# Cross-attention in halves between its projections, waits for half a weight, and one-hots ahead of a branch: one change to a whole-model kernel on one core

## The chip, the cores and the metric

The kernel runs on one core of a Trainium2 chip. The core has a matrix engine (PE, TensorE), three engines for element-wise work (DVE, VectorE; ACT, ScalarE; POOL, GpSimd), a queue engine that issues transfers here (SP, SyncE), and 16 DMA engines. The metric is the device time of one launch in microseconds; times of several launches are given as their median.

## The reference, cut to what matters

Two layers of a hybrid block, then one block with a mixture of experts, all in float32; 256 tokens of 1024 values.

```python
h = x
for l in range(2):
    mix = hybrid_mixer(h, ...)               # recurrence and windowed attention
    h = layer_norm(A * h + mix, ...)
    h = layer_norm(A * h + cross_attention(h, mem, cq_w[l], ckv_w[l], co_w[l]), ...)
    h = layer_norm(A * h + swiglu(h, ffn_wi[l], ffn_wo[l]), ...)

def cross_attention(u, mem, cq_w, ckv_w, co_w):      # 4 heads of 256, 256 rows of mem
    q = (u @ cq_w).reshape(B, S, 4, 256)
    k, v = split(mem @ ckv_w)
    s = einsum('bshd,bmhd->bhsm', q, k) * 256 ** -0.5
    o = einsum('bhsm,bmhd->bshd', softmax(s), v)
    return o.reshape(B, S, 1024) @ co_w

# second block, once
x = x + g_a * merge(neighbourhood_attention, spatial_gate) @ w_out
t = rms(x) * (1 + scale) + shift
# 4 groups of 4 experts: the best group, in it the two best experts, with their weights
for e in range(16):
    out += gate[:, e] * ((silu(t @ w1[e]) * (t @ w3[e])) @ w2[e])
x = x + g_f * out
```

## The kernel before

**Order of work.** Each engine has a `Queue`: the program appends instructions to it, and the order in which it appends them is the order in which the engine runs them. An instruction carries the tokens (semaphore values) that it waits for. So an engine that waits at one instruction holds back all behind it.

**Weights.** All weights stream in as units of 1 MB (128 rows of 2048 values) in the order of a plan (`stream_plan`). SP issues their transfers to three `raw` buffers as these come free (`emit_dma`, L304), and two more, `landing`, are added late. Products are made to float32 precision from two parts: `split_half` (L320) makes, for 1024 of the 2048 columns at a time, a high part on ACT (`whs`, a copy to a reduced type) and a low part on DVE (`wls`, the rest), so a unit takes two such halves, and there are three places for split units. Activations are kept in two parts too (`P0h`, `P0l`, `P1h`, `P1l`), and `mm3` makes one product out of three: high by high, high by low, low by high. When PE has used a unit, `release` (L377) frees its place and appends the next halves to ACT and DVE (`pump`), unless the state `slow` or `hold` is set. `take` gives a GEMM its unit with the token to wait for: up to here the tokens of both halves, from its first product on.

**GEMMs and side work.** `gemm_tm` (L474) and `gemm_fm` (L512) run over units and tiles. After each tile they call `tick` (L388), which steps a generator in the list `side`, if there is one; this is how other work is put between the tiles. With `slow` set it also appends one half of a weight (`feed`). `finish_side` runs what is left of the generators.

**Cross-attention** (`cross`, L1052). Queries come from the two GEMMs of `cq_w`, two heads each. The generator `attend` (L1072) has three steps: `scores(t, hp)` makes scores and softmax for the rows of half t and two heads, `turn(hd)` transposes the weights of a head, `weigh(hd)` sums the values and splits the result for `co_w`. Copies go to ACT and DVE in turn. Before, the generator is run to its end between `cq_w` and `co_w`:

```python
            for c in range(2):
                gemm_fm("cq_w", P0, N["t"], (2 * c, 2 * c + 1), q_evac(c), by_unit=True)
...
            at = attend()
            next(at)
            side.append(at)
            finish_side()
```

**Second block.** `merge_evac` (L1614) takes the second half of `w_out_2`, adds the residual and makes the normalized rows `xn_`, for which DVE waits for a power on POOL. `f_fm` transposes them and splits them for the router and the experts; in its `early` form it returns `low(n)`, which makes the low parts later. The router's logits and the choice of experts follow on all engines, and at the end of it the counts of tokens per expert, their offsets, and for each token its two places in the sorted rows (`first`, `second`). A flag then sets a branch: where no expert has more than 128 tokens, the sparse way (`sparse`, L1792) runs. In it `gather` (L1809) makes one-hot matrices `Pall` of the places, two instructions for each half of the tokens, and with 32 products in eight banks brings the tokens into the order of the experts. Then come `up` and `down` for each expert.

## Time and profile before

| | |
|---|---|
| runs | 1680.62 us median of 3 (1676.35 to 1683.83) |
| profiled execution | 1681.34 us, its span 1679.4 us |
| mean granted clock of PE | 0.981 |
| PE busy | 1596.6 us (95%), 8036 products |
| PE's weight loads | 1303.4 us (78%) |
| DVE busy | 1151.0 us (69%), 1617 instructions |
| ACT busy | 903.9 us (54%), 1377 instructions |
| POOL busy | 79.7 us (5%) |
| DMA | 339.35 MB, mean 202 GB/s |
| chain that ended last | PE 70%, DVE 15%, ACT 8%, DMA 3%, issue 3% |

A row of a timeline names the line that issues the instruction, often that of a helper: L199 is a product, L203 a transpose, L207 a copy or function on ACT, L211, L215 and L219 are element-wise work on DVE, L222 a reduction, L225 a copy on DVE. A product of two float32 operands that are not split (scores and sums) shows as two records. `bank` is one of the eight PSUM banks, `tail` and `arena` are shared regions (in the cross-attention keys and values, queries and softmax). The granted clock is a share of full speed, 2.4 GHz. The releaser behind an arrow is what the engine waited for last.

### The profile page before, as it was taken

What the parts mean: (1) busy time and instruction counts of PE and PEld (TensorE: products, weight loads), DVE (VectorE), ACT (ScalarE), POOL (GpSimd) and SP (SyncE); (2) the same over time, 40 slices, a digit from 0 to 9 for tenths busy, and PEclk for the clock granted to TensorE, in tenths of its full rate; (3) what the DMA queues carried; (4) which work ended last, traced back from release to release, by engine and by line L of the source; (5) the groups of instructions that cost most, each with busy time, mean ns of one, the idle gap of its engine ahead of it and who ended that gap; (6) DMA issues with size and microseconds to landing.
All of it is one profiled execution on the core that took longest, in us unless ns stands there. A gap on an engine that the chain in (4) does not pass through costs nothing.

```text
span 1679.4 us, 20455 instructions
## 1 busy us (share of the span) xinstructions
PE 1596.6 (95%) x8036; PEld 1303.4 (78%) x8036; DVE 1151.0 (69%) x1617; ACT 903.9 (54%) x1377; POOL 79.7 (5%) x75
## 2 busy tenths in 40 slices
PE   7999999989999999989999899999989969999997
PEld 7987788776888789878878667888767758777786
DVE  7457655657545584667566478866664669999997
ACT  5466443435444364764434254544353448888885
POOL 0010000001000000100000000000200000000005
PEclk9999999999999999999999999999999879999999
DMA  7445234535654454542356278874440318999995
GB/s 286 177 153 198 89 112 158 194 126 211 242 198 177 149 202 175 204 172 86 116 200 226 75 259 296 315 257 175 150 169 26 119 63 302 364 374 369 370 371 177
DMA packets 52202, 339.35 MB, mean 202 GB/s; under 512 B 7835, under 2 KB 8477, under 8 KB 13316
## 3 DMA queue, kind: packets, MB, share of 16 engines
q1 hardware_dynamic: 48932, 331.79, 53.7%
q0 software_dynamic: 3168, 6.20, 1.0%
q8 instruction: 65, 1.06, 0.3%
q14 instruction: 37, 0.30, 0.1%
HBM read 332.82 MB, written 10.49 MB: 204 GB/s over the span
## 4 chain that ended last, share of the span: by engine, by line
PE 70%; DVE 15%; ACT 8%; DMA 3%; issue 3%; POOL 1%; ACTq 0%; DVEq 0%; SPq 0%
PE bank L199 66%; DVE wls L211 6%; PE bank L203 4%; ACT whs L207 3%; DMA raw<-in_ws_dram 3%; ACT arena L208 1%; DVE arena L211 1%; DVE sm L222 1%; ACT P1h L1847 1%; DVE h L211 1%; DVE arena L219 1%; POOL sm L231 1%; DVE arena L844 1%; ACT arena L207 1%; DVE arena L215 1%
## 5 line engine op out<-in xcount | busy, mean ns | idle before, releaser
L211 DVE TENSOR_TENSOR wls<-raw,whs 128x1024 fp32r<-128x1024 f32 x442 | 523.5, 1227 | 243.4 <-ACT whs L207 242.8
L207 ACT ACTIVATE whs<-raw 128x1024 fp32r<-128x1024 f32 x442 | 443.2, 1051 | 276.1 <-PE bank L199 193.3
L199 PE MATMUL bank<-whs,P1h 128*128 128x512 f32 (+1 forms) x732 | 291.2, 398 | 5.2 <-DVE P1l L1849 2.0
L199 PE MATMUL bank<-whs,P1l 128*128 128x512 f32 (+1 forms) x732 | 285.5, 390 | 0.0
L199 PE MATMUL bank<-wls,P1h 128*128 128x512 f32 (+1 forms) x732 | 285.1, 390 | 0.0
L199 PE MATMUL bank<-whs,P0h 128*128 128x512 f32 (+1 forms) x640 | 257.6, 402 | 6.3 <-DVE P0l L211 2.5
L199 PE MATMUL bank<-whs,P0l 128*128 128x512 f32 (+1 forms) x640 | 250.2, 391 | 0.0
L199 PE MATMUL bank<-wls,P0h 128*128 128x512 f32 (+1 forms) x640 | 250.1, 391 | 0.0
L199 PEld LDWEIGHTS bank<-whs,P1h 128*128 128x128 f32 x732 | 138.4, 189 | 36.2 <-DVE P1l L211 3.6
L199 PEld LDWEIGHTS bank<-whs,P1l 128*128 128x128 f32 x732 | 138.3, 189 | 29.2
L199 PEld LDWEIGHTS bank<-wls,P1h 128*128 128x128 f32 x732 | 138.4, 189 | 26.9
L199 PEld LDWEIGHTS bank<-whs,P0h 128*128 128x128 f32 x640 | 122.1, 191 | 40.3 <-issue 6.7
L199 PEld LDWEIGHTS bank<-whs,P0l 128*128 128x128 f32 x640 | 121.7, 190 | 25.8
L199 PEld LDWEIGHTS bank<-wls,P0h 128*128 128x128 f32 x640 | 122.0, 191 | 23.9 <-issue 0.7
L207 ACT ACTIVATE arena<-bank 128x256 f32<-128x256 f32 (+1 forms) x131 | 59.8, 463 | 82.6 <-PE bank L199 67.6
L208 ACT ACTIVATE arena<-arena,sm 128x128 f32<-128x128 f32 (+2 forms) x80 | 40.1, 502 | 92.7 <-DVE sm L215 92.7
L203 PE MATMUL bank<-ident,arena 128*128 128x128 f32 x386 | 64.6, 287 | 19.9 <-DVE arena L225 8.7
L199 PE MATMUL bank<-P0h,whs 128*128 128x256 f32 x256 | 74.3, 290 | 4.1 <-DVE wls L211 4.1
L231 POOL TENSOR_TENSOR sm<-sm,mhalf 128x1 f32<-128x1 f32 (+1 forms) x30 | 24.3, 811 | 1089.8 <-DVE sm L215 952.4
L203 PEld LDWEIGHTS bank<-ident,arena 128*128 128x128 f32 x386 | 49.9, 151 | 31.8 <-ACT arena L207 8.4
L199 PE MATMUL bank<-P1h,whs 128*128 128x256 f32 x256 | 73.7, 288 | 0.0
L199 PE MATMUL bank<-P0h,wls 128*128 128x256 f32 x256 | 73.1, 286 | 0.0
(267 smaller groups left out, 2497.1 us busy)
## 6 DMA issues: line engine op xcount, KB each, us to landing
raw<-in_ws_dram SPq DMA_DIRECT2D x264, 1024.0 KB, 4.9
landing<-in_ws_dram SPq DMA_DIRECT2D x38, 1024.0 KB, 7.1
lnb<-in_ln_g_dram SPq DMA_DIRECT2D x6, 512.0 KB, 5.8
lnb<-in_ln_b_dram SPq DMA_DIRECT2D x6, 512.0 KB, 6.5
ydram<-arena POOLq DMA_DIRECT2D x4, 512.0 KB, 11.8
mid<-in_bias_dram SPq DMA_DIRECT2D x1, 2048.0 KB, 7.6
h<-in_x_dram SPq DMA_DIRECT2D x2, 512.0 KB, 4.0
lnb<-in_mem_dram SPq DMA_DIRECT2D x1, 1024.0 KB, 13.1
```

Of the source, the lines that this page charges most:

```text
L199: return PE.put(lambda e: e.matmul(out, lhsT, rhs, start=start, stop=stop, skip_group_check=skip), w, inc)
L203: return PE.put(lambda e: e.transpose(out, in_, ident[0:n, 0:n]), w, inc)
L207: return AC.put(lambda e: e.activation(out, in_, func, bias=bias, scale=scale), w)
L208: return AC.put(lambda e: e.activation(out, in_, func, bias=bias, scale=scale, accum_out=acc), w)
L211: return VE.put(lambda e: e.tensor_tensor(out, a, b, op), w)
L215: return VE.put(lambda e: e.tensor_scalar(out, a, s1, None, op0), w)
L219: return VE.put(lambda e: e.scalar_tensor_tensor(out, a, s, b, op0, op1), w)
L222: return VE.put(lambda e: e.tensor_reduce(out, a, AX.X, op), w)
L231: return GP.put(lambda e: e.tensor_tensor(out, a, b, op), w)
L844: v3 = VE.put(lambda e, k=k: e.tensor_tensor_scan(xc[:, k, :], ra[:, k, :], gi[:, k, :], 0.0, ALU.mult, ALU.add), [v2])
L1847: a = AC.put(lambda g, hi=hi, at=place_of: g.activation(hi, at(AC), ACT.Copy, bias=0.0, scale=1.0), [[T["all", k] for k in range(k0, k1)], ...
```

## The change

It has four parts.

1. **Start.** The first half of `x` is loaded ahead of the identity and the condition, the second half behind them.
2. **Halves of units.** A unit's token becomes two, and `half_of` gives a product that reads the first half of the unit the first token alone. All GEMMs use it.
3. **Cross-attention.** `attend` is in `side` while the second GEMM of `cq_w` runs, so the scores of the first two heads lie between its tiles. The rest is in another order, and the last two sums come behind the first tile of `co_w`.
4. **Router.** Two low parts of `f_fm` are appended in DVE's wait for POOL, with `hold` set until `f_fm` is done, and one more half of a weight is appended behind it. The four instructions for `Pall` stand ahead of the branch, the cast of the offsets behind them; `gather` makes the 16 products of the first half of the tokens first, which wait for its one-hots alone, then those of the second.

```diff
@@ split_half, take
-                split_tok[n] = [split_tok[n], tok]
+                split_tok[n] = [[split_tok[n]], [tok]]
...
+        def half_of(tok, kk, per):
+            return tok[0] if isinstance(tok, list) and 2 * kk < per else tok
...
+        xr = ins["x"].rearrange("a (t p) d -> p (a t) d", p=128)
+        c_h = [load(h[:, 0, :], xr[:, 0, :], s="d_h0")]
         c_ident = load(ident[:, :], ins["ident"], s="d_ident")
         c_cond = load(sm[:, 640:656], ins["cond"], s="d_cond")
-        xr = ins["x"].rearrange("a (t p) d -> p (a t) d", p=128)
-        c_h = [load(h[:, t, :], xr[:, t, :], s=f"d_h{t}") for t in range(2)]
+        c_h.append(load(h[:, 1, :], xr[:, 1, :], s="d_h1"))
@@ gemm_tm
-                            part(w, slice(None), kk), first, closes and kk == per - 1, tok,
+                            part(w, slice(None), kk), first, closes and kk == per - 1, half_of(tok, kk, per),
...
@@ cross
-            for c in range(2):
-                gemm_fm("cq_w", P0, N["t"], (2 * c, 2 * c + 1), q_evac(c), by_unit=True)
-            xfree = PE.last()
...
-                for hp in range(2):
-                    for t in range(2):
-                        scores(t, hp)
-                        if t:
-                            yield
+                for t in range(2):
+                    scores(t, 0)
+                    yield
+                yield
                 turn(0)
                 turn(1)
+                for t in range(2):
+                    scores(t, 1)
+                for hd in range(2):
+                    weigh(hd)
+                    oT[0].append(X[("o", hd)])
+                turn(2)
+                turn(3)
                 yield
-                for hd in range(2, 6):
-                    weigh(hd - 2)
-                    if hd < 4:
-                        turn(hd)
-                    if hd % 2:
-                        yield
-
+                for hd in range(2, 4):
+                    weigh(hd)
+                    oT[1].append(X[("o", hd)])
+                yield
+
+            oT = [[], []]
+            gemm_fm("cq_w", P0, N["t"], (0, 1), q_evac(0), by_unit=True)
+            finish_side()
             at = attend()
-            next(at)
             side.append(at)
-            finish_side()
+            gemm_fm("cq_w", P0, N["t"], (2, 3), q_evac(1), by_unit=True)
+            xfree = PE.last()
...
             gemm_tm("co_w", src, lambda i: i, res_evac(rs, 0))
+            finish_side()
@@ merge_evac, router
+                    if t:
+                        fT[0][2](0)
                     xn_[t] = ts(xs[:, t, :], h[:, t, :], smv(o + 5, 1), None, ALU.mult, None, g, Q["ph"])
+                    if t:
+                        fT[0][2](1)
+                        state["slow"], state["hold"] = False, True
...
-        for n in range(2):
-            fT[0][2](n)
         fT = [fT[0][0], f_fm(1, False)[0]]
+        state["slow"], state["hold"] = True, False
...
-        feed(2)
+        feed(3)
...
-        v_off = vcopy(offi[:, :], begins, d_)
...
         v_place = tt(second, second, first, ALU.subtract, a_, d_)
+        p_at = []
+        for t in range(2):
+            p_ = ts(Pall[:, t, :], count, first[:, t:t + 1], None, ALU.is_equal, None, n_, v_place, Q["ph"])
+            p_at.append(stt(Pall[:, t, :], count, second[:, t:t + 1], f32(Pall[:, t, :]), ALU.is_equal, ALU.add, p_))
         v_slot = ts(slot, slot, -1.0, None, ALU.add, None, v, v_place)
+        v_off = vcopy(offi[:, :], begins, v_slot)
@@ gather
-                for t in range(2):
-                    p_ = ts(Pall[:, t, :], count, first[:, t:t + 1], None, ALU.is_equal, None, n_, v_place, start)
-                    p_ = stt(Pall[:, t, :], count, second[:, t:t + 1], f32(Pall[:, t, :]), ALU.is_equal, ALU.add, p_)
...
                 for k in range(8):
-                    for i in range(4):
-                        t, p = i // 2, i % 2
-                        m = mm(banks[k][:, :], rows[p][:, t, k * 128:(k + 1) * 128], Pall[:, t, :], i == 0, i == 3,
-                               p_, rows_tok, bankfree[k], inc=(i == 3))
+                    for p in range(2):
+                        mm(banks[k][:, :], rows[p][:, 0, k * 128:(k + 1) * 128], Pall[:, 0, :], p == 0, False,
+                           p_at[0], rows_tok, bankfree[k])
+                for k in range(8):
+                    for p in range(2):
+                        m = mm(banks[k][:, :], rows[p][:, 1, k * 128:(k + 1) * 128], Pall[:, 1, :], False, p == 1,
+                               p_at[1], inc=(p == 1))
```

On PE, before, this stands between the last products of `cq_w` (names with P1) and the first of `co_w` (names with P0): four score blocks of four products, then transposes and sums in turn.

```order
L199 MATMUL bank<-P1l,whs 128x256
L199 MATMUL bank<-P1h,wls 128x256
L199 MATMUL bank<-tail,arena 128x256 x16
L203 MATMUL bank<-ident,arena 128x128 x8
L199 MATMUL bank<-arena,tail 128x256 x4
L203 MATMUL bank<-ident,arena 128x128 x4
L199 MATMUL bank<-arena,tail 128x256 x4
L203 MATMUL bank<-ident,arena 128x128 x4
L199 MATMUL bank<-arena,tail 128x256 x8
L199 MATMUL bank<-whs,P0h 128x512
```

Two of these blocks have moved ahead of this place, and two of the four sums behind it, as the next pieces show.

In the changed kernel the first score block stands on PE behind the first tile of `cq_w`'s second GEMM, and the second block stands likewise one tile later.

```order
L199 MATMUL bank<-P1l,whs 128x256
L199 MATMUL bank<-P1h,wls 128x256
L199 MATMUL bank<-tail,arena 128x256 x4
L199 MATMUL bank<-P1h,whs 128x256
L199 MATMUL bank<-P1l,whs 128x256
```

A block that stood behind the GEMM is now inside it, and the GEMM's other tiles come behind it.

Behind that GEMM the two other score blocks stand between two pairs of transposes, with the first two sums ahead of the second pair.

```order
L199 MATMUL bank<-P1l,whs 128x256
L199 MATMUL bank<-P1h,wls 128x256
L203 MATMUL bank<-ident,arena 128x128 x8
L199 MATMUL bank<-tail,arena 128x256 x8
L199 MATMUL bank<-arena,tail 128x256 x8
L203 MATMUL bank<-ident,arena 128x128 x8
L199 MATMUL bank<-whs,P0h 128x512
```

Eight products of scores and eight of sums are left here. The eight other products of sums now stand after the first 12 products of `co_w`.

On DVE, in the cross-attention of layer 0 (L225 `arena<-bank` copies queries, `wls` is the low half of a weight, L222, L215 and L228 belong to one softmax), the softmaxes of the first two score blocks have moved ahead among the weight halves.

```order
 L225 COPY arena<-bank 128x512
-L211 TENSOR_TENSOR wls<-raw,whs 128x1024 x4
-L225 COPY arena<-bank 128x512
-L211 TENSOR_TENSOR wls<-raw,whs 128x1024 x2
+L211 TENSOR_TENSOR wls<-raw,whs 128x1024 x2
+L222 TENSOR_REDUCE sm<-bank 128x2
+L215 TENSOR_SCALAR sm<-sm 128x2
+L228 RECIPROCAL sm<-sm 128x2
+L215 TENSOR_SCALAR arena<-arena,sm 128x256 x2
+L211 TENSOR_TENSOR wls<-raw,whs 128x1024 x2
+L222 TENSOR_REDUCE sm<-bank 128x2
+L215 TENSOR_SCALAR sm<-sm 128x2
```

Each softmax now has a pair of weight halves ahead of it on DVE.

On DVE, at the end of the router, this is the difference from the flag on (`Pall` are the one-hots; L2071 and L2073 read the flag and branch).

```order
 L222 TENSOR_REDUCE sm<-sm 128x2 x2
 L211 TENSOR_TENSOR sm<-sm 128x2
-L215 TENSOR_SCALAR sm<-sm 128x32
-L2071 TENSOR_LOAD flag
-L2071 ISA x2
-L2073 COMPARE_AND_BRANCH
 L215 TENSOR_SCALAR Pall<-arena,sm 128x512
 L219 SCALAR_TENSOR_TENSOR Pall<-arena,sm,Pall 128x512
 L215 TENSOR_SCALAR Pall<-arena,sm 128x512
 L219 SCALAR_TENSOR_TENSOR Pall<-arena,sm,Pall 128x512
+L215 TENSOR_SCALAR sm<-sm 128x32
+L225 CAST offi<-sm 128x16
```

The one-hots, which stood behind the branch, stand ahead of the last small operation and of the cast of the offsets, which the branch now follows.

## Rows read from the trace of the kernel before

**Rows 1.** PE's waits. Engine, buffer, line <- releaser: us in all, times, longest.

```profile
PE bank L199 <- ACT arena L207: 6.1, 2, 3.0
PE bank L199 <- DVE wls L211: 6.0, 5, 4.1
PE bank L199 <- DVE Pall L219: 5.7, 1, 5.7
PE bank L199 <- ACT arena L208: 5.5, 4, 2.1
```

**Rows 2.** Timeline, SP at the start: start us, us, instruction, xcount.

```profile
0.73 0.40 SPq L245 DMA_DIRECT2D ident<-in_ident_dram  x1
...
1.66 0.90 SPq L245 DMA_DIRECT2D h<-in_x_dram  x2
```

**Rows 3.** Timeline, PE at the start; [idle before <-releaser].

```profile
5.23 1.94 PE L203 MATMUL bank<-ident,h 128*128 128x128 f32 x8 [5.23 <-DMA h<-in_x_dram]
...
13.88 0.55 PE L199 MATMUL bank<-P0h,whs 128*128 128x256 f32 x1 [4.12 <-DVE wls L211]
```

**Rows 4.** Timeline, DVE at the start.

```profile
11.38 5.77 DVE L211 TENSOR_TENSOR wls<-raw,whs 128x1024 fp32r<-128x1024 f32 x5 [0.25 <-ACT whs L207]
```

**Rows 5.** Timeline, ACT at the start.

```profile
14.83 2.00 ACT L207 ACTIVATE whs<-raw 128x1024 fp32r<-128x1024 f32 x2 [0.48 <-DMA raw<-in_ws_dram]
```

**Rows 6.** Timeline, PE in the cross-attention of layer 0.

```profile
344.40 0.28 PE L199 MATMUL bank<-P1l,whs 128*128 128x256 f32 x1
344.52 0.28 PE L199 MATMUL bank<-P1h,wls 128*128 128x256 f32 x1
344.64 3.62 PE L199 MATMUL bank<-tail,arena 128*128 128x256 f32 x16
...
354.81 1.04 PE L203 MATMUL bank<-ident,arena 128*128 128x128 f32 x8
358.88 3.53 PE L199 MATMUL bank<-arena,tail 128*128 128x256 f32 x8 [3.04 <-ACT arena L207]
...
364.86 3.73 PE L199 MATMUL bank<-arena,tail 128*128 128x256 f32 x16
368.24 0.58 PE L199 MATMUL bank<-whs,P0h 128*128 128x512 f32 x1
368.66 0.39 PE L199 MATMUL bank<-wls,P0h 128*128 128x512 f32 x1
```

**Rows 7.** Timeline, DVE in the cross-attention of layer 0.

```profile
336.45 0.69 DVE L225 COPY arena<-bank 128x512 f32<-128x512 f32 x1
...
348.27 0.69 DVE L222 TENSOR_REDUCE sm<-bank 128x2 f32<-128x512 f32 x1
...
350.98 0.69 DVE L222 TENSOR_REDUCE sm<-bank 128x2 f32<-128x512 f32 x1
```

**Rows 8.** Timeline, PE in the cross-attention of layer 1.

```profile
920.41 3.62 PE L199 MATMUL bank<-tail,arena 128*128 128x256 f32 x16
```

**Rows 9.** Timeline, DVE in the cross-attention of layer 1.

```profile
912.68 0.68 DVE L225 COPY arena<-bank 128x512 f32<-128x512 f32 x1
```

**Rows 10.** Timeline, PE at the border of two units, feed-forward of layer 0.

```profile
456.29 0.39 PE L199 MATMUL bank<-whs,P1l 128*128 128x512 f32 x1
456.52 0.39 PE L199 MATMUL bank<-whs,P0h 128*128 128x512 f32 x1
```

**Rows 11.** Timeline, PE in the gather (its 1st and 14th product).

```profile
1373.49 0.80 PE L199 MATMUL bank<-Pall,P0h 128*128 128x512 f32 x1 [5.70 <-DVE Pall L219]
...
1379.21 0.40 PE L199 MATMUL bank<-Pall,P0l 128*128 128x512 f32 x1
```

**Rows 12.** Timeline, DVE from the router to the one-hots.

```profile
1369.69 0.16 DVE L211 TENSOR_TENSOR sm<-sm 128x2 f32<-128x2 f32 x1
...
1370.98 0.49 DVE L215 TENSOR_SCALAR Pall<-arena,sm 128x512 fp32r<-128x512 f32 x1 [0.91 <-DVE sm L215]
```

**Rows 13.** Timeline, ACT ahead of the router.

```profile
1354.50 1.51 ACT L207 ACTIVATE arena<-bank,sm 128x128 f32<-128x128 f32 x4 [2.57 <-DVE P1l L211]
```

**Rows 14.** Windows: us, busy (xcount) PE, PEld, DVE, ACT, POOL; PEclk, DMA share, GB/s.

```profile
360.00:369.00 9.00, 9.00 (x42) 7.52 (x41) 2.67 (x4) 2.66 (x5) 0.00 (x0) 0.89 0.00 0
...
1374.00:1386.00 12.00, 10.02 (x33) 7.63 (x32) 6.38 (x20) 4.45 (x7) 0.00 (x0) 0.78 0.01 1
```

15 lines of the change are left out of this document (8 added, 7 removed).

## The prediction

> **What bounds the kernel now.** I read the table of engines first, then PE's waits, then the timelines of the places that the diff touches. PE is busy for 1596.6 of 1679.4 us, so the change can win only where PE stands still (82.8 us) or runs at the low clock. The reader should see in PE's waits that no single one is large and that the diff goes to four of the larger: `wls` 6.0, `Pall` 5.7, and `arena` from ACT 6.1 and 5.5, both inside the two cross-attentions [rows 1]. With the 5.2 at the very start [rows 3] that is 28.5 us, the most that could go. In the feed-forward and the experts PE runs nearly without a gap, so what is saved ahead of them is saved at the end.
>
> **Start.** SP issues the identity at 0.73 and the first half of `x` as its third transfer, at 1.66 [rows 2]. PE waits for `x` until 5.23 [rows 3], 3.57 after the issue. Issued first, at 0.73, it is there at 4.30: 0.93 earlier. The identity goes out some half a microsecond later and, being much smaller, is not what is late.
>
> PE's first product is at 13.88, after a wait of 4.12 for the low half of the first weights [rows 3]. DVE makes five such halves in 5.77, from 11.38 [rows 4]: one every 1.13. With the wait halved, PE goes on after the first of them, 1.13 earlier; six products then cover the second. ACT's first wait for a weight DMA is at 14.83, for the third unit [rows 5], so nothing shows that the 0.93 is lost to a DMA; if the first unit landed only when ACT took it, it is. Ends: 0 and 2.1. I take 2.1, as no row shows such a wait.
>
> **Cross-attention, twice.** Before, four score blocks, four transposes and four weighted sums stand alone between two GEMMs. In layer 0 PE starts them at 344.64 and reaches `co_w` at 368.24, in 23.6 [rows 6]. In it PE waits 5.8, which is half of 6.1 + 5.5 [rows 1], and the first weighted sum takes 3.53 where two later ones take 3.73 together [rows 6]: 1.65 lost to the low clock. So 7.4 at most can be won per layer.
>
> After, two score blocks stand inside the second `cq_w` GEMM. They push its end back by the 3.62 that they take [rows 6]; call that end T'. A new wait comes in: the first block needs all queries of the first GEMM, and DVE copies the last of them only at 336.45, for 0.69 [rows 7], behind layer-norm work. The second GEMM is 96 products of 0.12 [rows 6], so it starts at 333.1, and its first quarter ends at 336.0. PE waits 1.1 there. In layer 1 the same reckoning from 920.41 gives 911.8, against a copy that ends at 913.4 [rows 8, 9]: 1.6. Behind this wait stand the other three quarters of the GEMM.
>
> From T', DVE first makes two weight halves, done 3.6 after T' (as 348.27 is to 344.64 [rows 6, 7]), then a copy of 0.69, then two softmaxes of 2.71 (348.27 to 350.98 [rows 7]): T' + 9.7. PE meanwhile has two transposes (1.04 [rows 6]), two score blocks (3.62) and two weighted sums (3.73): T' + 8.4. So it waits 1.3 for the softmax, transposes (1.04), and waits 0.4 more, because the splits of the two sums (0.69 each) stand behind that softmax on DVE. `co_w` starts at T' + 11.2, does one tile (2.75), does the last two sums (3.73), and goes on at T' + 17.7. Before, that point lay at 23.6 + 2.75 = 26.4 after the old end of the GEMM; now it lies at 3.62 + 1.1 + 17.7 = 22.4: 4.0 saved. In layer 1 the longer first wait leaves 3.5. **Together 7.5**, between 0 and 14.8 (no wait left, no slow sum). The weight splits that now stand between the softmaxes wait for the same GEMM as before; they are ahead of their use by a unit, so their shift costs nothing.
>
> **Weights by halves elsewhere.** Apart from the start, four waits for `wls` are left, 6.0 - 4.1 = 1.9 in sum [rows 1]. The first half is there 1.13 before the second, so most of it goes. I take 1.5 of 0 to 1.9, as some of them stand ahead of an attention stage that waits for ACT in any case. The change adds 100 waits on PE ahead of the branch, and almost none behind it. A wait that is already met costs nothing that can be seen: at the border of two units, where the names change from P1 to P0 and a wait stands, the products stay 0.23 apart [rows 10]. So I cost these at nothing; if PE's stream didn't cover them, rival 4 says what they take. The Trainium skill, "TensorE: Matmul & The Clock Gate", puts into the table at its head that PE pulls weight loads ahead of products that still run, and prices 128 columns at an estimated 0.107 us (section on LDWEIGHTS). A load that must wait for its own half can't be pulled ahead, so by that rule 100 waits would give back 10.7, the sum would be 2.5 instead of 13.2, and the time 1678; the rows at the border speak against it.
>
> **Router and one-hots.** PE waits 5.70 for the four one-hot instructions and begins the gather at 1373.49 [rows 11]. DVE has their inputs at 1369.69 + 0.16, does one small operation, crosses the branch (0.91), and makes them from 1370.98 on [rows 12], in 2.5 for four. After, they follow at once, from about 1369.8 (the cast of the offsets, a tenth, now comes behind them), and the gather needs only two of the four to begin: 1371.0 to 1371.1, which is 2.4 earlier. The other two are done 1.25 later, and 16 products stand between. Against this stands a moved split. Two low parts go into DVE's wait for POOL, and ACT need not wait 2.57 for them [rows 13]; the evacuation of the second transposes starts some 0.6 earlier. But one weight half, 1.0 on ACT, now stands ahead of the copies of the router's logits, and ACT has no gap from there on: the logits come 0.3 to 0.4 later. Net 2.1, between 0.3 and 2.5. The gate sums on DVE now come behind the one-hots and the branch; they end about when the first copy of the gather is wanted, so I cost them at nothing, and at a copy's 0.7 if they are late.
>
> **Sum.** 2.1 + 7.5 + 1.5 + 2.1 = 13.2. The profiled execution took 1681.34, so it would take 1668.1. It stands 0.7 above the median of the runs, 1680.62, so I forecast **1667.4**. About 0.5% (8.4 us) is what a measurement of this kernel can tell from no change.
>
> **Rivals.**
>
> 1. *The softmax is not hidden.* If in each layer one more unit's split (two halves, 2.3) and a copy (0.7) get in ahead of the second softmax, 3 are lost twice, the cross-attentions give 1.5, and the time is 1673.4. For it: ACT and DVE work in order, and these splits wait for PE. Against it: the first two softmaxes have two or three quarters of a GEMM, 5.8 to 8.6, before their use.
>
> 2. *The start is set by a DMA.* Then the 2.1 become 0 to 1.1, and the time 1668.4 to 1669.5. For it: the wait at 14.83 [rows 5]. Against it: it is the third unit that waits.
>
> 3. *The clock.* After a wait PE's products can come at half the rate: from 1373.49 the gather's first 13 steps take 5.7, 0.44 each instead of 0.23 [rows 11], at a mean granted clock of 0.78 [rows 14]. The change swaps one large gap for three smaller ones in each cross-attention. If each of the six is followed by 3.5 us (the slow sum [rows 6]) to 5.7 us at 1.2 GHz, half of that is lost each time, 10 to 17 in all: 1678 to 1685. **Slower than before** from 13.2 on, which is 2.2 for each gap. Against it: the old gaps were 5.8 in 10.6 us and left the clock at 0.89 behind them [rows 14]; the new ones are 1.1 to 1.6, 1.3 and 0.4, with 6 to 10 us of work between them.
>
> 4. *A wait inside a tile holds PE up.* The most that a first product costs in the rows is one step of 0.42 instead of 0.23 after other work (368.24 to 368.66 [rows 6]). At 0.19 for each of the 100 waits that is 19, and the time 1686; slower than before from 0.13 each. Against it: the border of two units [rows 10].
>
> **How the numbers follow.** The forecast has 0.63, rival 1 0.15, rival 2 0.10, rival 3 0.08, rival 4 0.04. Faster by over 0.5% means under 1672.2: most of the forecast's spread, rival 2 and a little of rival 1 make 0.69. Within 0.5%: most of rival 1, the low ends of 3 and 4, and the tail of the forecast, 0.25. Slower by over 0.5% needs 21.6 more than forecast, which is rivals 3 and 4 together or something that no row shows: 0.06. The range goes from 1661 (cross-attentions at 11 and the router at its end, with the runs' scatter of 3 below the median) to 1678 (rival 1, and the low end of rival 3).
>
> **What would show it.** PE's first product of weights lies near 11.8. In each cross-attention PE no longer waits for ACT's `arena`; it waits 1 to 1.6 ahead of the first score block and about 1.3 ahead of the third transpose. One wait for `Pall` of 3 to 3.5 is left instead of 5.7, and of the waits for `wls` about 3, at the start. The prediction would be wrong with score blocks that wait over 3 inside the GEMM, a granted clock under 0.85 in a cross-attention, steps over 0.3 inside weight tiles, or a gather whose evacuation waits for the gate sums.

## The result

| | before | change |
|---|---|---|
| median, with the ratio of the change to before | 1678.81 us (4 runs) | 1660.8 us (4 runs), 0.9888, interval 0.9859 to 0.9918 |
| the same, measured again (e12 below) | 1676.65 us (17 runs) | 1661.36 us (6 runs), 0.9895, interval 0.9872 to 0.9918 |
| profiled execution, its span | 1681.34, 1679.4 us | 1661.53, 1659.7 us |
| PE idle, span less busy time | 82.8 us | 68.5 us |

The change is faster by 1.1%, some 18 us; 13.2 were forecast, and the time lies just under the lower end of the range, 1661.0; the second measurement lies just inside it. These two rows of the page of the changed kernel answer to the table shown of before.

```profile
span 1659.7 us, 20348 instructions
...
PE 1591.2 (96%) x8036; PEld 1303.7 (79%) x8036; DVE 1149.8 (69%) x1617; ACT 903.1 (54%) x1377; POOL 79.9 (5%) x75
```

PE's waits of the changed kernel, in us in all, times and longest:

```profile
PE bank L203 <- DVE arena L215: 8.2, 4, 4.7
...
PE bank L203 <- DMA ident<-in_ident_dram: 4.2, 1, 4.2
...
PE bank L199 <- DVE Pall L219: 3.2, 1, 3.2
PE bank L199 <- DVE wls L211: 2.9, 1, 2.9
...
PE bank L203 <- DMA h<-in_x_dram: 1.2, 1, 1.2
```

Of the four waits in [rows 1], the two of the cross-attentions are gone, and `wls` and `Pall` have become one shorter wait each, as the forecast said. The first wait, 5.2 for `x`, is now 4.2 for the identity. New are 1.6 for the last softmax of each cross-attention (in the 8.2, which before were 4.6), and 1.2 for the second half of `x`.

To see where time goes, I lined up PE's instructions of each profile with those of before and took, at each place, how much earlier the same product starts. The table gives the growth of that lead (negative: time saved) from place to place, places in the time of before. The columns e1 to e5 are the experiments below; a stretch whose program an experiment leaves alone is a control.

| stretch of before | change | again (e12) | e1 start | e2 halves | e3 cross | e4 router | e5 experts |
|---|---|---|---|---|---|---|---|
| to 14, first weights | -1.64 | -1.81 | -0.57 | -1.24 | +0.06 | -0.06 | +0.24 |
| 312 to 390, cross-attention 0 | -3.89 | -5.25 | -0.04 | +0.15 | -5.33 | +0.14 | +0.06 |
| 390 to 689 | -0.55 | -0.49 | -0.06 | -0.58 | +0.06 | -0.09 | +0.17 |
| 689 to 874 | +3.38 | +3.43 | -0.08 | +1.53 | +2.97 | +1.02 | +1.54 |
| 888 to 968, cross-attention 1 | -5.37 | -5.37 | +0.10 | -0.14 | -5.17 | -0.07 | -0.02 |
| 968 to 991 | -1.36 | -1.37 | -0.52 | -1.38 | +0.01 | -0.47 | -0.52 |
| 991 to 1050 | -2.63 | -2.68 | -2.50 | -2.66 | +1.73 | -2.48 | -1.99 |
| 1050 to 1186 | -1.02 | -1.02 | 0.00 | -1.03 | 0.00 | 0.00 | 0.00 |
| 1186 to 1333 | -0.48 | -0.45 | -0.19 | -0.94 | -0.85 | -0.06 | -4.38 |
| 1333 to 1373, router | -2.06 | -2.02 | -0.02 | -0.20 | -0.08 | -1.98 | -0.22 |
| 1373 to 1390, gather, first expert | -2.06 | -2.08 | -0.02 | -0.04 | +0.04 | -2.03 | -0.09 |
| 1390 to 1671, experts | -1.98 | -1.78 | +0.33 | -1.97 | -0.18 | +0.10 | -1.81 |
| all else | +0.03 | -0.06 | -0.47 | +0.12 | -0.08 | -0.23 | -0.30 |
| whole, to 1671 | -19.63 | -20.95 | -4.04 | -8.38 | -6.82 | -6.21 | -7.32 |

Three lines are not the change's. From 991 to 1050 most kernels are 2.0 to 3.2 ahead of before, e4 and e5 among them, whose program is that of before up to 1300. There the one profiled execution of before lost time: DVE waited 1.39 for a weight.

```profile
1034.15 2.33 DVE L219 SCALAR_TENSOR_TENSOR arena<-raw,sm,arena 128x512 f32<-128x512 f32 x3 [1.39 <-DMA raw<-in_ws_dram]
```

In e1 DVE does not wait there. From 1186 to 1333 e5 gains 4.38 where it has nothing changed: over these 147 us the mean granted clock was 0.95 in its profile and 0.92 in that of before. And the loss from 689 to 874, where the diff changes only which half of a weight is waited for, is the clock's too. These are two windows of before, then the same of the change, with the granted clock in the column behind POOL:

```profile
745.00:775.00 30.00, 25.87 (x138) 20.57 (x137) 19.77 (x33) 16.00 (x45) 0.00 (x0) 0.94 0.22 74
815.00:835.00 20.00, 18.20 (x95) 14.98 (x94) 10.23 (x15) 6.99 (x10) 0.00 (x0) 1.00 0.31 108
```

```profile
745.00:775.00 30.00, 25.88 (x137) 20.80 (x137) 19.16 (x36) 14.59 (x42) 0.00 (x0) 0.89 0.27 104
815.00:835.00 20.00, 18.19 (x84) 14.81 (x84) 9.93 (x14) 8.89 (x12) 0.00 (x0) 0.91 0.30 110
```

Lower by 0.05 for 30 us and by 0.09 for 20, the clock takes some 3.3 us, which is the loss. Kernels without the new cross-attention have part of it: e2, 0.89 and 1.00, loses 1.5. What makes the clock fall there stays open. So a difference of two profiled executions means something only at a place that moves in every kernel with the edit and in none without it.

### The profile page after: what moved, and what is told of

The parts are those of the page before. It is cut to its first block, busy times and chain, and to the rows that moved or that the text cites. A ratio compares the mean times of both kernels' runs of the same rounds, so it can differ in the third digit from the quotient of the medians.

```text
span 1659.7 us, 20348 instructions
## 1 busy us (share of the span) xinstructions
PE 1591.2 (96%) x8036; PEld 1303.7 (79%) x8036; DVE 1149.8 (69%) x1617; ACT 903.1 (54%) x1377; POOL 79.9 (5%) x75
## 4 chain that ended last, share of the span: by engine, by line
PE 72%; DVE 17%; ACT 6%; DMA 2%; issue 2%; POOL 1%; SPq 0%; DVEq 0%; ACTq 0%
PE bank L199 68%; DVE wls L211 7%; PE bank L203 4%; ACT whs L207 2%; DMA raw<-in_ws_dram 2%; DVE h L211 1%; DVE arena L211 1%; ACT arena L208 1%; DVE sm L222 1%; POOL sm L231 1%; DVE arena L219 1%; DVE arena L849 1%; DVE arena L215 0%; ACT arena L207 0%; ACT L207 0%
```

## The experiments

### The four parts, each alone

The edits are the parts of the diff above, each put alone into the kernel before.

**e1, start.**

> Only the order of the loads at the start is changed. Theory A (each part is worth what its own place shows): PE's first transposes start near 4.2 instead of 5.23 and the first product of weights near 13.0 to 13.4 instead of 13.88, so 0.5 to 1.0 us are gained, ratio 0.9994 to 0.9997, which no timing can tell from 1. Rival B (the second half of x, now issued fourth, takes the gain back): the first product of weights stays within 0.3 of 13.88.

Measured: ratio 0.9991 (0.9975 to 1.0007). The first transposes start at 4.29, where PE now waits for the identity, and the second half of `x` is waited for by 0.87; the first product of weights comes at 13.31, 0.57 earlier. Theory A.

**e2, halves.**

> Only the waits for half a unit are put in. Theory A (place by place): the wait ahead of the first product of weights falls from 4.1 to 2.9 to 3.0, the four other waits for wls (1.9 in sum) go but are mostly met again at the next wait for an activation; the stage of the experts ends as many us after its first product as before, within 0.5; 1.5 to 3 us in all. Rival B (half waits are what shortens the expert stage by 2.0 and the stretch 980 to 1050 by 3.5 in the changed kernel): 5 to 8 us, with the expert stage 2.0 shorter. Rival C (100 more waits cost PE): slower than before by 5 or more, steps over 0.3 inside tiles.

Measured: ratio 0.9974 (0.9959 to 0.9990). By the table 1.24 at the start, 1.38 from 968 to 991 (0.5 of it in the controls too), 1.03 from 1050 to 1186, and 1.97 in the experts, to which 0.58 from 390 to 689 come. Theory A's "within 0.5" for the experts falls. Rival C falls: the first product of a second half, in the middle of a tile, keeps the step of 0.23. Rival B was right on the experts and wrong on 991 to 1050, which is an accident of before. Why half waits help in the experts is left to e5 and e13.

**e3, cross-attention.**

> Only the cross-attention is changed. Theory A: PE's waits in the two cross-attentions fall from 11.6 to 4 to 5 (the softmax of the last two score blocks 1.6, a split 0.4, each twice, and a query copy) and the slow weighted sum at 358.88 is gone: from the start of cq_w to the feed-forward 4 to 5.5 us less in each layer, 8 to 11 in all, ratio 0.9935 to 0.995. The stretch 980 to 1050 and the experts stay as before within 1. Rival B (the transfers that follow layer 1 come earlier against PE, so the 3.5 us of waits between 980 and 1050 go with this part): 12 to 14 us, ratio 0.992.

Measured: ratio 0.9952 (0.9934 to 0.9970). 5.33 and 5.17 are saved, 10.5 in all, within Theory A. Rival B falls, as 991 to 1050 does not shorten here; it is 1.73 longer, at a granted clock of 0.97 instead of 1.00.

**e4, router.**

> Only the low parts, the one-hots ahead of the branch and the order of the gather are changed. Theory A (the wait and the clock): PE's wait for Pall falls from 5.7 to 3.2, and the clock comes back within the gather, so the first expert's first products come at 0.23 and not at 0.43 as before: 4 to 5 us, ratio 0.997 to 0.9976. Rival B (the wait alone): 2 to 2.6 us, with steps of 0.43 behind the gather as before. Rival C: the expert stage behind it, where the transfers were busy 96% of the time, takes back what comes ahead of it: under 1 us at the end.

Measured: ratio 0.9984 (0.9969 to 1.0000). PE waits 3.2 for `Pall`; 1.98 are saved up to the gather, and 2.03 more up to the first expert. Theory A by the trace, and Rival C falls: what is saved ahead of the experts is still there at the end. The ratio is worth 2.7 us, with an interval from 0 to 5, and tells neither from Rival B. Windows of before (the gather's slow part, its rest with the wait behind it, the first expert) and of the change show the clock in the column behind POOL:

```profile
1373.40:1379.20 5.80, 5.71 (x13) 4.46 (x14) 3.64 (x19) 0.78 (x2) 0.00 (x0) 0.50 0.01 3
1379.20:1385.70 6.50, 4.53 (x20) 3.38 (x18) 2.94 (x5) 3.37 (x6) 0.00 (x0) 1.00 0.00 0
1385.70:1389.30 3.60, 3.58 (x9) 2.86 (x10) 3.57 (x5) 2.43 (x4) 0.00 (x0) 0.55 0.00 0
```

```profile
1357.90:1361.40 3.50, 3.50 (x8) 2.81 (x9) 2.35 (x10) 0.00 (x0) 0.99 (x2) 0.50 0.00 0
1361.40:1369.60 8.20, 5.95 (x25) 4.46 (x23) 5.60 (x18) 4.11 (x7) 0.00 (x0) 0.97 0.00 0
1369.60:1373.20 3.60, 3.54 (x15) 2.92 (x16) 3.60 (x6) 2.79 (x5) 0.00 (x0) 1.00 0.02 5
```

Before, PE stood still 5.7, then ran at 0.50 of full speed (1.2 GHz) for 5.8, and after the next wait, 2.0, it was granted 0.55 on the mean of 3.6 us. With the change it stands still 3.2 and runs at 0.50 for 3.5; after a next wait of 2.3 it is at full speed (2.4 GHz). The second slow stretch is there in every kernel with the old one-hots (before, e1, e2, e3, e5, e6, e13, e14) and in none with the new ones (change, e4, e7 to e12, e15, e16).

### What the router's part consists of

**e9, one-hots alone.** Added to before: the four instructions ahead of the branch; the gather as it was.

```diff
+            p_at.append(stt(Pall[:, t, :], count, second[:, t:t + 1], ...))   # ahead of the branch
...
                         m = mm(banks[k][:, :], rows[p][:, t, ...], Pall[:, t, :], i == 0, i == 3,
-                               p_, rows_tok, bankfree[k], inc=(i == 3))
+                               p_at[1], rows_tok, bankfree[k], inc=(i == 3))
```

> The kernel before with the one-hots ahead of the branch alone; the gather in its old order, waiting for all four of them, and no low parts. Theory A (the clock behind the gather depends on how long PE stood still ahead of it): the wait for Pall falls from 5.7 to 4.4 to 4.5, and the slow stretch behind the first expert's wait (1.7 to 2.0 us in the kernel before, gone in the four kernels with the whole change of the router) stays, so 1.2 us. Rival B (what clears it is that the products come in another order or earlier against something else): the slow stretch goes here too, 2.9 to 3.2 us.

Measured: ratio 0.9979 (0.9966 to 0.9993). Theory A falls on the clock: the wait is 1.3 shorter, as it said, but the slow stretch at the first expert is gone too, and 2.62 more are saved up to there. The windows are the gather's start and the first expert:

```profile
1369.90:1373.00 3.10, 3.10 (x7) 2.47 (x8) 1.84 (x12) 0.60 (x1) 0.99 (x2) 0.50 0.02 5
1381.10:1385.40 4.30, 4.28 (x19) 3.56 (x20) 4.08 (x6) 3.61 (x6) 0.00 (x0) 1.00 0.13 19
```

The ratio is worth 3.5 us, with an interval from 1.2 to 5.7, so the effect is the one of Rival B. But the order of the products is not what clears the second slow stretch. What has changed ahead of it is the length of the first standstill, 4.4 instead of 5.7, and of the slow stretch behind it; whether that is the cause, or that the products come earlier against something else, stays open.

**e7, without the low parts.** The change, but these lines as before:

```diff
-                    if t:
-                        fT[0][2](0)
...
+        for n in range(2):
+            fT[0][2](n)
...
-        feed(3)
+        feed(2)
```

> The changed kernel with the low parts and the weight half ahead of the router put back as before (two halves of a weight there, low parts behind the normalized rows). Theory A (the moved half costs more than the low parts give: 0.39 gained, 0.89 lost in the trace of the changed kernel): the first product of the gather comes 0.4 to 0.6 earlier, counted from the start of w_out_2's second half, and the time is 0.5 under the changed kernel's. Rival B (the low parts are worth the 0.6 that the prediction gave them, and the half is needed ahead of the gather): 0.3 to 1.5 over the changed kernel's.

Measured: ratio 0.9907 (0.9887 to 0.9927), 1661.44: the change's time. By the leads, low parts and moved half give 0.43 ahead of the router, take 0.86 in it, and give back 0.35 in the gather and 0.6 behind it: 0.5 for the change in all. That is near what a stretch wanders by where nothing is changed (-0.2 to +0.3 in the experts), and no timing can tell it, so neither theory is settled.

**e8, two orders changed.** The change with the second half of `x` third and two halves of a weight ahead of the router:

```diff
-        c_cond = load(sm[:, 640:656], ins["cond"], s="d_cond")
         c_h.append(load(h[:, 1, :], xr[:, 1, :], s="d_h1"))
+        c_cond = load(sm[:, 640:656], ins["cond"], s="d_cond")
...
-        feed(3)
+        feed(2)
```

> The changed kernel with the second half of x issued ahead of the condition, and with two halves of a weight ahead of the router instead of three (low parts as in the change). Theory A: PE's wait for the second half of x falls from 1.2 to 0.7 to 0.8, the router's logits come 0.9 earlier as ACT has one copy of 1.0 less ahead of them, and the unit whose half is left out is not needed until the first experts, whose wait for P1l is longer: 1.0 to 1.4 us under the changed kernel's time. Rival B (the half that is left out is met again by the first expert, which waits for it): 0.4 under it, all of it from the start.

Measured: ratio 0.9912 (0.9896 to 0.9929), and the start lost 1.2: the lead at the first product of weights is 0.42 instead of 1.64. Both theories missed ACT: its first instruction works on the condition, and now waits for that transfer until 7.05, with the copies of the first transposes queued behind it.

```profile
7.05 0.21 ACT L207 ACTIVATE sm<-sm 128x16 f32<-128x16 f32 x1 [5.04 <-DMA sm<-in_cond_dram]
7.17 1.07 ACT L207 ACTIVATE P0h<-bank 128x512 fp32r<-128x512 f32 x2
```

The missing half of a weight brings the logits 0.7 earlier; 0.4 of it is left at the first expert and 0.2 at the end.

### The cross-attention

**e6, sums ahead of co_w.** As e3, without the step between the transposes and the last sums:

```diff
                 turn(2)
                 turn(3)
-                yield
                 for hd in range(2, 4):
                     weigh(hd)
```

> As e3_cross, but all four weighted sums stand ahead of co_w. Theory A (the scores inside the GEMM hide the first softmax, and the late sums hide only the copy of the last transposes and the split of the first sums): the wait of 1.6 for the softmax stays, a new wait of 0.7 to 1.2 comes ahead of the third sum, and each layer gives 0.7 to 1.2 less than in e3_cross: 6 to 7.5 us where that gave 9 to 10 by its trace. Rival B (the late sums are most of the gain, as they give DVE time to split): 3 us in all, ratio 0.998.

Measured: ratio 0.9958 (0.9945 to 0.9972). 5.51 and 5.33 are saved, as much as in e3. Both theories fall: ahead of the third sum PE waits 0.25, not 0.7 to 1.2, and the 0.41 for the split ahead of `co_w` is gone. The late sums are worth nothing here, and the whole gain is that the first two score blocks lie in the GEMM and the rest is in another order.

**e10, query copies on ACT.**

```diff
-                    X[("q", f // 2)] = copy_by(j, qT[:, f:f + 2, :], ps, m, mend)
+                    X[("q", f // 2)] = copy_by(j if c else 0, qT[:, f:f + 2, :], ps, m, mend)
```

> The changed kernel with both query copies of cq_w's first GEMM on ACT. Theory A (the term of the query copy: only the second head's half of the first score block waits for DVE's copy): the first score block takes 1.54 from its start to the next tile in both layers, as the second one does, instead of 1.9 and 1.4 with a wait of 0.4; 0.4 in each layer, 0.8 in all, which no timing can tell. Rival B (ACT's copy comes later than DVE's, or holds up a weight half): the block waits 0.5 or more.

Measured: the first block takes 1.54 in both layers, without a wait. Theory A. The ratio, 0.9877 (0.9857 to 0.9896), lies within the interval of the change's.

**e11, weight halves behind the softmax.** e10 and:

```diff
                 for t in range(2):
                     scores(t, 0)
                     yield
+                state["hold"] = True
                 yield
...
                 turn(2)
                 turn(3)
+                state["hold"] = False
+                pump()
                 yield
```

> As e10, and the two weight halves that stand between the query copies and the third softmax come behind the last transposes. Theory A (these halves, 2.4 us on DVE, are why PE waits 1.6 for the last softmax): this wait falls to 0 to 0.4, the wait for the split (0.4) stays, and the slow stretch behind it in layer 0 (1.7 in the changed kernel) goes: 2.5 to 3.5 us under e10, near 1657. Rival B (the halves are then late for co_w's second unit or the splits of the last sums stand behind them): a new wait of 1 to 2 in co_w, and no gain.

Measured: ratio 0.9869 (0.9850 to 0.9888), 1655.9. Theory A for the waits: the one for the softmax falls from 1.61 to 0.20, that for the split stays at 0.41, and the layers save 7.28 and 7.45, which is 3.0 and 1.6 more than in e10. By the medians it is only 1.0 under e10 (1656.93), with intervals that overlap. PE at the third transpose, first in the change, then in e11:

```profile
356.63 0.88 PE L203 MATMUL bank<-ident,arena 128*128 128x128 f32 x6 [1.61 <-DVE arena L215]
357.92 0.47 PE L199 MATMUL bank<-whs,P0h 128*128 128x512 f32 x1 [0.41 <-DVE P0l L211]
358.23 0.51 PE L199 MATMUL bank<-wls,P0h 128*128 128x512 f32 x1
358.54 0.63 PE L199 MATMUL bank<-whs,P0l 128*128 128x512 f32 x1
358.96 0.63 PE L199 MATMUL bank<-whs,P0h 128*128 128x512 f32 x1
```

```profile
357.56 0.88 PE L203 MATMUL bank<-ident,arena 128*128 128x128 f32 x6 [0.20 <-DVE arena L215]
358.85 0.47 PE L199 MATMUL bank<-whs,P0h 128*128 128x512 f32 x1 [0.41 <-DVE P0l L211]
```

In the change the products of `co_w` behind these waits come 0.43 apart for a while (358.54 to 361.52), in e10 too; in e12 and e11 they come 0.23 apart. Its first tile takes 4.42 in the change and 2.84 in e12 (357.92 to 362.34, and 357.74 to 360.58), so 1.6 is lost, which is why the two profiles of the change differ in cross-attention 0. As e12 is the same program as the change, nothing shows that the edit of e11 clears this slow stretch. Between 14 and 312, ahead of its edit, the profile of e11 loses 2.7, with a granted clock of 0.93 instead of 0.97 from 160 to 210.

### Half waits or fewer conditions

**e5, half waits in the experts alone.**

> Waits for half a unit in the experts alone, up and down; all ahead of the branch as before. Theory A (the 2.0 us that the expert stage is shorter with half waits, 0.3 at each of seven places, come from the products of an expert that use a unit whose second half DVE has just made): 2.0 us from the first expert's first product to the end, nothing ahead of it, ratio 0.9988. Rival B (the expert stage is shorter because the units come into it earlier after all that was saved ahead): no change behind the first expert, ratio 1.000.

Measured: the expert stage is 1.81 shorter, with nothing ahead of it changed, so Theory A has the place. By timing it can't be told: ratio 1.0001 (0.9989 to 1.0012). But the cause it gives is wrong. The products that start sooner are the first of an expert's second stage, `whs,Pall`, and in both kernels what comes last for them is DVE's split of the hidden rows; the unit's halves are earlier instructions of DVE. In before DVE ends that split at 1450.11:

```profile
1449.69 0.42 DVE L211 TENSOR_TENSOR Pall<-bank,Pall 128x256 fp32r<-128x256 f32 x1
```

PE starts the product 0.25 later, 0.44 after the one ahead of it:

```profile
1449.92 0.39 PE L199 MATMUL bank<-whs,P1l 128*128 128x512 f32 x1
1450.36 0.47 PE L199 MATMUL bank<-whs,Pall 128*128 128x512 f32 x1
```

With half waits alone DVE ends the split at 1444.44, and PE starts 0.10 later, 0.28 after the product ahead:

```profile
1444.26 0.39 PE L199 MATMUL bank<-whs,P1l 128*128 128x512 f32 x1
1444.54 0.47 PE L199 MATMUL bank<-whs,Pall 128*128 128x512 f32 x1
```

The trace's semaphore records, which the timeline leaves out, show what stands between. Before, two separate wait instructions stand ahead of this product on PE's weight-load queue, one with one condition and one with two; with half waits there is none, and the load of the product's weights carries the wait itself. Over the whole run the separate wait instructions of PE fall from 258 to 151 in the change, which are the 107 instructions that its page counts less (20348 instead of 20455), though 100 products more have a wait.

Is it the conditions or the instructions that cost? Three other products of the stage have one separate wait in both kernels, with two conditions in before and with one in e5. The step is the same, 0.32 to 0.35. The first of them, before and with half waits:

```profile
1415.40 0.39 PE L199 MATMUL bank<-whs,P1l 128*128 128x512 f32 x1
1415.72 0.47 PE L199 MATMUL bank<-whs,Pall 128*128 128x512 f32 x1
```

```profile
1409.89 0.39 PE L199 MATMUL bank<-whs,P1l 128*128 128x512 f32 x1
1410.21 0.47 PE L199 MATMUL bank<-whs,Pall 128*128 128x512 f32 x1
```

So the price goes with the number of separate wait instructions, not with their conditions.

**e13, the condition alone.** In before, the latest token first, so that the older values of the same semaphore need no wait:

```diff
-                                part(w, slice(None), k, cols_), i == 0 and k == 0, i == 1 and k == 1, tok,
-                                T["hT", c], bankfree[b] if i == 0 and k == 0 else None, inc=(k == 1))
+                                part(w, slice(None), k, cols_), i == 0 and k == 0, i == 1 and k == 1, T["hT", c],
+                                tok, bankfree[b] if i == 0 and k == 0 else None, inc=(k == 1))
```

> The kernel before; only in an expert's second product the tokens stand in another order: the transposed hidden rows (DVE's latest value) first, the unit's halves, which are older values of the same semaphore, behind it, so that they need no wait of their own. PE waits for the whole unit as before. Theory W (a product that PE stands at pays 0.15 for a second condition in the wait ahead of it, and half waits gave 2.0 in the experts because they left one condition out): the expert stage is 1.5 to 2.2 shorter, as in e5, nothing ahead of it changes. Theory H (the half wait itself gave it, as PE need not wait for the second half): no change, within 0.3.

Measured: 2.30 from the first expert on, more than with half waits, and no half is waited for. Theory H falls. DVE ends the split at 1445.02, and the product starts 0.05 later, at a step of 0.24, next to the bare 0.23:

```profile
1444.83 0.39 PE L199 MATMUL bank<-whs,P1l 128*128 128x512 f32 x1
1445.07 0.50 PE L199 MATMUL bank<-whs,Pall 128*128 128x512 f32 x1
```

So where the operand is only just ready, two separate waits cost the step 0.21, one 0.10 to 0.12, and none 0.05 (e5) or 0.01 (e13, which has no separate wait there either); ten products of the stage read so in each of the three kernels, and three more, of before and e5, have the one. What sets 0.05 against 0.01 is open. A separate wait that was met long before costs nothing: before, 108 of 120 products of 512 columns behind one keep the step of 0.23. The time, ratio 0.9994 (0.9977 to 1.0010), can't show 2 us.

**e14, merged in before; e15, in the change; e16, in the best.** One value for each semaphore:

```diff
+    def flat(self, tokens, most):      # the latest value of each semaphore
...
     def wait(self, tokens):
-        for t in tokens:
...
-            sem, value = t
+        for sem, value in self.flat(tokens, {}).values():
```

> The kernel before, with the tokens of an instruction merged to one value for each semaphore, everywhere; PE's separate wait instructions fall from 350 to 62 (half waits alone: 185), ACT's from 400 to 326. Theory W: the expert stage 1.5 to 2.5 shorter, and where half waits alone had gained, at 968 to 991 (0.9) and 1050 to 1186 (1.0), this kernel gains nothing or little, as no half is waited for there; 2 to 4 us in all. Theory H: nothing in the expert stage, 0 to 1 us in all.

> The changed kernel with merged tokens; PE's separate wait instructions fall from 182 to 60. Theory W: most of those on PE's path went with the half waits, so 0.3 to 1.5 us under the changed kernel, in places with several producers (gather, router, attention). Theory H: the same time as the changed kernel within 0.5 in every stretch that the clock leaves alone.

> As e11 (query copies on ACT, weight halves behind the softmax), with merged tokens. Theory W: 0.3 to 1.5 under e11, ratio to the kernel before 0.985 to 0.988; Theory H: the ratio of e11, 0.987, within its interval.

Measured: e14 ratio 0.9973 (0.9963 to 0.9983), as much as half waits (0.9974) without one half wait: 2.44 in the experts, and 1.37 from 968 to 991, where Theory W expected little, but only 0.10 from 1050 to 1186 and nothing at the start. So of what half waits gave, the experts and most of 968 to 991 are fewer separate waits; the start and 1050 to 1186 are the half that needn't be waited for. On the change (e15, 0.9906, 0.9886 to 0.9926) and on e11 (e16, 0.9878, 0.9858 to 0.9897) merging is worth nothing that shows.

### The change again

**e12.**

> The changed kernel again, beside these. Theory A (the parts add up: 1.5 + 4.4 + 8.0 + 2.7 by the medians of the four parts alone): 15 to 18 us under the kernel before, ratio 0.9893 to 0.9911, and in the trace the first expert's products come at 0.23 from the start. Rival B (the profiled execution of the change was itself a lucky one): under 14 us, and the stretches that differ from the first profile are those of the clock.

Measured: ratio 0.9895 (0.9872 to 0.9918), 15.3 by the medians; the parts alone gave 0.6, 3.9, 6.0 and 1.9 by their own medians, 12.4, or by their ratios 1.5 + 4.4 + 8.0 + 2.7 = 16.6. Theory A, to within the intervals, which are some 3 us either way for each part. The profile differs from the first in the clock alone, by 1.4 in cross-attention 0.

## Why the prediction was wrong

It had the direction, and undershot by 5 us by the first measurement, by 2 to 4 by the second. Three of its steps failed: the wait for the query copy in the cross-attention, the price of met waits in the term of the halves, and the clock behind the gather, which it put at nothing. By its own steps:

- **Start, 2.1: measured 1.6 to 1.8.** The half wait gave what was said: PE waits 2.92 instead of 4.12. Of the 0.93 only half arrived. The first transposes come 1.04 earlier, but what they wait for is now the identity, which the prediction held to be "not what is late", and the second half of `x`, issued fourth, makes PE wait 1.19:

```profile
4.19 1.97 PE L203 MATMUL bank<-ident,h 128*128 128x128 f32 x8 [4.19 <-DMA ident<-in_ident_dram]
7.35 1.97 PE L203 MATMUL bank<-ident,h 128*128 128x128 f32 x8 [1.19 <-DMA h<-in_x_dram]
12.24 0.58 PE L199 MATMUL bank<-P0h,whs 128*128 128x256 f32 x1 [2.92 <-DVE wls L211]
```

- **Cross-attention, 7.5: measured 9.3 and 10.6 in the two profiles of the change.** The stretch behind the GEMM was worked out well: 1.61 for the softmax (1.3 forecast), 0.41 for the split (0.4), and `co_w` starts 11.06 after T' (11.2). The step that failed is the new wait for the query copy, "the first block needs all queries of the first GEMM". Only its second head does; for the first, ACT's copy is enough, and that ends at 329.5. In layer 0 the block begins while DVE's copy of the last queries still waits its turn; in layer 1 its second half waits 0.37:

```profile
328.87 0.60 ACT L207 ACTIVATE arena<-bank 128x512 f32<-128x512 f32 x1
334.43 2.25 PE L199 MATMUL bank<-tail,arena 128*128 128x256 f32 x8
334.82 0.68 DVE L225 COPY arena<-bank 128x512 f32<-128x512 f32 x1
...
910.50 1.13 PE L199 MATMUL bank<-tail,arena 128*128 128x256 f32 x4 [0.37 <-DVE arena L225]
```

  From its start to the next tile the block takes 1.90 to 2.01 in layer 0 and 2.14 to 2.18 in layer 1, against 1.54 without the wait (e10), so the wait costs 0.4 and 0.6 instead of 1.1 and 1.6. The other 0.5 in each layer is mainly that two sums were put at 3.73, the time from first start to last end. From start to start they take 3.27; two score blocks, put at 3.62, and the first sums take 3.46 and 3.45, but being ahead of the softmax's wait they only lengthen it:

```profile
347.73 3.62 PE L199 MATMUL bank<-tail,arena 128*128 128x256 f32 x16
351.19 3.62 PE L199 MATMUL bank<-arena,tail 128*128 128x256 f32 x16
354.64 0.38 PE L203 MATMUL bank<-ident,arena 128*128 128x128 f32 x2
...
362.34 3.62 PE L199 MATMUL bank<-arena,tail 128*128 128x256 f32 x16
365.61 0.58 PE L199 MATMUL bank<-whs,P0h 128*128 128x512 f32 x1
```

  With these the sum comes to some 5.3 and 5.1, near the 5.3 of e3 and e12 in layer 0 and the 5.2 to 5.4 in layer 1. Layer 0 of the first profile gave 3.9, as a slow stretch followed the waits there (granted clock 0.72 from 357 to 363, 1.00 in e12). e8 has such a stretch in both layers and gives 3.75 and 3.74, so the clock decides on 1.5 for each layer.

- **Weights by halves elsewhere, 1.5: measured some 4.4** (0.5 to 0.6, 0.9, 1.0 and 2.0, by the rows 390 to 689, 968 to 991 less its control, 1050 to 1186 and experts). This term failed by its cause. "A wait that is already met costs nothing that can be seen" was read at a border of two units, where the wait had long been met. Where another operand is only just ready, two separate waits cost 0.21, though the halves of the unit among their conditions had been met before. The diff left such instructions out (258 to 151) where the prediction counted only waits added, and 1.8 to 2.0 came from the experts, where it saw "almost none".
- **Router, 2.1: measured 2.0**, with the wait 2.5 shorter, the low parts 0.4 ahead of it (0.6 forecast), and the moved half 0.9 against it (1.0 forecast); the logits come 0.4 later, as it said.
- **The clock.** The sum had no term for it. The prediction saw the 13 slow steps of the gather and used them for a rival alone; that the first expert was slow too, and would not be behind a shorter standstill, is the 2.06 that it left out: 0.8 from the shorter slow stretch in the gather and 1.6 at the first expert, less 0.3 for a longer wait between (2.3 instead of 2.0).
- **The base.** The median of before was 1680.62 by three runs, and 1676.65 to 1677.19 beside the experiments (17 to 31 runs each). Some 3.5 of the 6.6 between the forecast time and the measured one are this.

Against the gains stands the loss of 3.4 from 689 to 874, which the prediction had not. It is the granted clock (see the windows behind the table), and it comes in three sizes: in that stretch before and e1 ran 3.4 us at 1.2 GHz, e2, e4 to e11, e13, e14 and e16 6.8, the change in both profiles, e3 and e15 10.2. Half of the excess, 1.7 and 3.4, is what most of these lost (1.0 to 2.0, and 3.0 to 3.5); e6 and e7, which ran 6.8, lost only 0.0 and 0.4. So the new cross-attention is not what brings it about, or not alone, and what does was not tried.

**The rivals.** The softmax is hidden but for 1.6 in each layer, not the two times 3 of rival 1. No weight transfer sets the start (rival 2), though PE's first two waits are for the identity and `x`: in the change ACT takes the first unit right behind its copies, at 9.87, without a wait for its transfer. Rival 3 shows at one of its six places, with 1.6, in one of the two profiles of the change. Rival 4 is refuted by e2: 100 more products with a wait, and 4.4 us faster, though at the same time the separate waits became fewer; of 237 products of 512 columns whose load alone carries the wait, 216 keep the step of 0.23 to 0.24. The Trainium skill, "TensorE: Matmul & The Clock Gate" (table at its head, and LDWEIGHTS), states that PE pulls weight loads ahead, and a price for a load. That a load that waits can't be pulled ahead, and the 10.7 that 100 such waits would give back, the prediction inferred from it; e2 shows nothing of this.

## What to carry to other kernels

When a wait is split or moved, count the separate wait instructions in front of the products whose operand is only just ready, not the waits in the program: name the latest value of a semaphore first, or merge values, so that older ones need no wait. When work moves ahead of its operands, ask operand by operand which copy it needs, and take distances from start to start, not busy times. And before a difference of two profiled executions is explained, look at the same stretch in a kernel that leaves it alone.

## What was not expected of the hardware

- A wait that is met is not always free: from the end of the last operand to the start of the product 0.25 passed with two separate wait instructions ahead of it, 0.14 to 0.15 with one, and 0.10 (e5) or 0.05 (e13) with the wait on the product's own load. Waits met long before showed no such price.
- A standstill of 5.7 was followed by two slow stretches, the second behind a further wait of 2.0 and 6.5 us of mostly full clock; one of 3.2 or 4.4 by one, though the further wait was as long (before against e9 and the change).
- The order of four transfers at the start set the time of work that needs none of those swapped: ACT's copies of the first transposes stood behind an instruction on 128 x 16 values that waited for its own transfer (e8).

The fastest version by its median is e11, 1655.9, with 0.9869 (0.9850 to 0.9888) of before; its interval overlaps that of the change, and that it is faster than the change rests on the two layers, 7.3 and 7.5 us instead of 3.9 to 5.3 and 5.4.
